# Stick-breaking heads: the value halves held in the array, both halves of the turned weights moving in one matmul

## The reference

```python
def stick_breaking_attention(q, k, v, g):
    scale = SB_HEAD_DIM ** -0.5                      # 64 ** -0.5
    for start in range(0, S, Q_BLOCK):               # blocks of 128 queries
        end = start + Q_BLOCK
        qb, kb, vb = q[:, start:end], k[:, :end], v[:, :end]
        z = jnp.einsum('bqhd,bkhd->bhqk', qb, kb).astype(jnp.float32) * scale
        mask = jnp.arange(end)[None, :] < (start + jnp.arange(Q_BLOCK))[:, None]
        log_1mb = jnp.where(mask, jax.nn.log_sigmoid(-z), 0.0)
        suffix = lax.cumsum(log_1mb, axis=3, reverse=True) - log_1mb
        a = jnp.where(mask, jnp.exp(jax.nn.log_sigmoid(z) + suffix), 0.0)
        outs.append(jnp.einsum('bhqk,bkhd->bqhd', a.astype(vb.dtype), vb))
    o = jnp.concatenate(outs, axis=1)
    return rmsnorm(o, g).reshape(B_, S, SB_WIDTH)
```

## Time and profile before

| what | value |
|---|---|
| median of 3 runs | 3962.36 us |
| lowest and highest | 3954.04 and 3963.06 us |
| span of the profiled execution | 3954.2 us |
| PE busy, share of the span | 3727.1 us, 94% |
| weight loads of PE | 3270.0 us, 83% |
| DVE busy | 1989.4 us, 50% |
| ACT busy | 1700.0 us, 43% |
| POOL busy | 799.3 us, 20% |
| chain that ended last: PE, DVE, ACT | 71%, 12%, 8% |

### The profile page before, as it was taken

How to read it: one execution, slowest core, us unless ns; L and a number is a source line. 1 busy time by engine, 2 the same in 40 slices (tenths; PEclk the granted TensorE clock), 3 DMA queues, 4 the chain that set the end, 5 groups by cost and what they waited for, 6 DMA issues and landing times.

```text
span 3954.2 us, 56218 instructions
## 1 busy us (share of the span) xinstructions
PE 3727.1 (94%) x21768; PEld 3270.0 (83%) x21768; DVE 1989.4 (50%) x4259; ACT 1700.0 (43%) x3455; POOL 799.3 (20%) x704
## 2 busy tenths in 40 slices
PE   7999899999998999999999999999999989999998
PEld 6888788787878887888888987888879987888897
DVE  4446575556646565555646545444566743101343
ACT  4334455556644444445544434334555543111322
POOL 3443333454444331100001000111000000000100
PEclk9999999999999999999999999999999999999999
DMA  6886667676666567454444555555353445555453
GB/s 171 276 270 184 191 206 276 223 266 233 241 238 210 208 208 277 173 174 165 164 171 159 176 192 208 181 181 179 132 201 124 142 157 212 192 192 191 163 187 143
DMA packets 327706, 774.76 MB, mean 196 GB/s; under 512 B 36241, under 2 KB 212369, under 8 KB 271122
## 3 DMA queue, kind: packets, MB, share of 16 engines
q1 hardware_dynamic: 266386, 731.31, 53.2%
q10 hardware_dynamic: 61056, 39.86, 3.6%
HBM read 591.49 MB, written 179.59 MB: 195 GB/s over the span
## 4 chain that ended last, share of the span: by engine, by line
PE 71%; DVE 12%; ACT 8%; issue 3%; DMA 2%; ACTq 2%; POOL 1%; SPq 0%; DVEq 0%
PE PS L1325 19%; PE PS L1327 19%; PE PS L1326 19%; PE PS L1447 3%; PE PS L1433 3%; PE PS L1425 2%; PE PS L1424 2%; PE PS L1449 2%; DVE PT L1967 1%; POOL WF L2225 1%; DVE SM L1935 1%; ACT WF L1547 1%; DVE BIG L1866 1%; ACT PT L1662 1%; ACT BIG L1604 1%
## 5 line engine op out<-in xcount | busy, mean ns | idle before, releaser
L1325 PE MATMUL PS<-WF,BIG 128*128 128x256 f32 (+1 forms) x2328 | 731.8, 314 | 21.1 <-POOL WF L2225 10.5
L1326 PE MATMUL PS<-WF,BIG 128*128 128x256 f32 (+1 forms) x2328 | 715.2, 307 | 0.0
L1327 PE MATMUL PS<-WF,BIG 128*128 128x256 f32 (+1 forms) x2328 | 714.9, 307 | 0.0
L1325 PE MATMUL PS<-BIG,WF 128*128 128x512 f32 (+1 forms) x1792 | 692.3, 386 | 20.4 <-DVE BIG L1866 9.5
L1327 PE MATMUL PS<-BIG,WF 128*128 128x512 f32 (+1 forms) x1792 | 677.7, 378 | 0.0
L1326 PE MATMUL PS<-BIG,WF 128*128 128x512 f32 (+1 forms) x1792 | 677.0, 378 | 0.0
L2225 POOL TENSOR_TENSOR WF<-RAW,WF 128x512 fp32r<-128x512 f32 x380 | 506.9, 1357 | 769.9 <-ACT WF L1547 769.7
L1967 DVE TENSOR_TENSOR PT<-PS,PT 128x512 fp32r<-128x512 f32 (+3 forms) x320 | 194.9, 609 | 616.3 <-ACT PT L1662 615.3
L1325 PEld LDWEIGHTS PS<-WF,BIG 128*128 128x128 f32 x2328 | 453.2, 195 | 48.6 <-POOL WF L2225 9.4
L1326 PEld LDWEIGHTS PS<-WF,BIG 128*128 128x128 f32 x2328 | 453.8, 195 | 22.4 <-issue 2.4
L1327 PEld LDWEIGHTS PS<-WF,BIG 128*128 128x128 f32 x2328 | 453.0, 195 | 18.9
(11 more groups left out here) (220 smaller groups left out, 6809.1 us busy)
## 6 DMA issues: line engine op xcount, KB each, us to landing
WF<-scratch_WS SPq DMA_DIRECT2D x264, 1024.0 KB, 5.1
scratch_WS<-WF SPq DMA_DIRECT2D x110, 1024.0 KB, 6.6
W<-scratch_WS SPq DMA_DIRECT2D x66, 1024.0 KB, 5.0
RAW<-in_w_in SPq DMA_DIRECT2D x84, 512.0 KB, 4.5
KV<-scratch_KS SPq DMA_DIRECT2D x60, 512.0 KB, 6.0
KV<-scratch_VS SPq DMA_DIRECT2D x60, 512.0 KB, 4.7
QQ<-scratch_QS SPq DMA_DIRECT2D x192, 128.0 KB, 4.9
XH<-in_x SPq DMA_DIRECT2D x32, 512.0 KB, 6.3
```

Source lines behind the costliest of these rows:

```text
L1325: pe.matmul(o, Ah, Bh, start=first, stop=False)
L1326: pe.matmul(o, Ah, Bl, start=False, stop=False)
L1327: return pe.matmul(o, Al, Bh, start=False, stop=last)
```

## The change

In the stick-breaking heads the two halves of the values (high, low, 64 columns each, so 128 columns of one head) become the stationary operand, and the two halves of the turned weights move in one matmul of 256 columns. PS[7] then holds, for head r, the output turned: 128 rows (64 of the high values, 64 of the low) by 256 columns (128 queries by the high weights, 128 by the low). So a tile's end gets three steps in place of one: `fold_out` (DVE) adds the two column halves into 256 columns of `PP`, `turn_out` (PE) turns them back with two transposes into PS[6], and `take_turned` (DVE) adds the two halves of the values into `OB`. The turned-back output comes two halves (`FB`) after the fold. The slot of `PP` that the fold writes to is taken from the ring of the logs (seven slots to six). All four products of the halves are now in the sum, three before. The values of the last block are stored with the head outermost, with eight DMAs of 64-column runs in place of four of 128-column runs.

```diff
+FB = 2
@@ attention()
+        fold_after = [(), ()]
@@ weigh(c, x, r, en)
-                _, o_before = oring.take(("o2", c, x["j"], x["qt"]))
-            do(("pv", c, x["x"], r, x["j"], x["qt"], x["kb"], x["w"], x["s"], vslot[c, x["j"], x["kb"]], en, x["first"],
+                _, o_before = oring.take(("o2" if en == 128 else "of", c, x["j"], x["qt"]))
+            do(("pv" if en == 128 else "pv_sb", c, x["x"], r, x["j"], x["qt"], x["kb"], x["w"], x["s"], vslot[c, x["j"], x["kb"]], en, x["first"],
...
                 if x["last"]:
-                    (take_out(c, x, r, en) if c == 0 else in_halves(1, lambda: take_out(c, x, r, en), True))
+                    take = take_out if en == 128 else fold_out
+                    (take(c, x, r, en) if c == 0 else in_halves(1, lambda: take(c, x, r, en), True))
...
+        def fold_out(c, x, r, en):
+
+            j, qt = x["j"], x["qt"]
+            do(("fold_out", c, x["x"], r, j, qt, fold_after[qt % 2]))
+            fold_after[qt % 2] = (("ot", c, j, qt),)
+
+            def turn_back():
+                _, before = tring.take(("o2", c, j, qt))
+                do(("turn_out", c, j, qt, before))
+                do(("take_turned", c, j, qt, ob_after[j % 2]))
+                if qt == 3:
+                    in_halves(1, lambda: finish_head(c, j))
+            in_halves(FB, turn_back)
...
-            aslot, cslot = Ring(7, pch.held[:7]), Ring(3, pch.held[7:])
+            aslot, cslot = Ring(6, pch.held[:6]), Ring(3, pch.held[7:])
+            fold_after[0] = fold_after[1] = pch.held[6]
...
-            pch = Ring(10, aslot.held + cslot.held)
+            pch = Ring(10, aslot.held + [fold_after[0] + fold_after[1]] + cslot.held)
@@ tensor_program(pe)
+            def pv_sb(c, x, r, j, qt, kb, w, s, vs, en, first, last, o_before):
...
+                vv = values_of(vs).rearrange("p (t r m) -> p t r m", t=4, r=2)
+                pp = turned_both(s)
+                o = PS[7][:, 256 * r:256 * r + 256].rearrange("p (a q) -> p a q", a=2)
+                for i in range(w // 128):
+                    m = pe.matmul(o, vv[:, i, r, :], pp[:, :, 128 * i:128 * i + 128],
+                                  start=first and i == 0 and r == 0, stop=last and i == w // 128 - 1, skip_group_check=True)
+                m.then_inc(*inc("weighed", ("pv", x, r)))
+
+            def turn_out(c, j, qt, before):
+                on.wait_ge("of", c, j, qt)
+                for e in before:
+                    on.wait_ge(*e)
+                for r in range(2):
+                    m = pe.transpose(PS[6][:, 128 * r:128 * r + 128], folded(qt)[:, 128 * r:128 * r + 128], ident)
+                m.then_inc(*inc("o_turned", ("ot", c, j, qt)))
@@ scalar_program, put_v
-                        act.dma_start(VS[ft + f, c, :, 2 * g:2 * g + 2, a, :], view.bitcast(F32)).then_inc(*landed(f"s_st{s}", ("qst", u)))
+                        if ft < 4:
+                            act.dma_start(VS[ft + f, c, :, 2 * g:2 * g + 2, a, :], view.bitcast(F32)).then_inc(*landed(f"s_st{s}", ("qst", u)))
+                            continue
+                        by_head = VS[ft + f, c, :, :, :, :].rearrange("p t a e -> p (t a e)").rearrange("p (t r a e) -> p t r a e", t=4, r=2, a=2)
+                        for i in range(2):
+                            act.dma_start(by_head[:, 2 * g + i, :, a, :],
+                                          view[:, i, :].rearrange("p (r e) -> p r e", r=2).bitcast(F32)).then_inc(*landed(f"s_st{s}", ("qst", u)))
@@ vector_program
+            def fold_out(c, x, r, j, qt, before):
+                dst = folded(qt).rearrange("p (r q) -> p r q", r=2)
+                src = PS[7][:, :].rearrange("p (r a q) -> p r a q", r=2, a=2)
+                on.wait_ge("pv", x, r)
...
+                dve.tensor_reduce(dst, src.rearrange("p r a q -> p r q a"), AX, ALU.add).then_inc(*inc("o_step", ("of", c, j, qt)))
+
+            def take_turned(c, j, qt, O_before):
+                dst = outs_of(j)[:, 128 * qt:128 * qt + 128].rearrange("p (r e) -> p r e", r=2)
+                src = PS[6][:, 0:256].rearrange("p (r a e) -> p r a e", r=2, a=2)
+                on.wait_ge("ot", c, j, qt)
...
```

23 lines of the change are left out of this document (18 added, 5 removed).

## The result

The changed kernel takes **4049.4 us** (median of 4 runs, 4046.4 to 4053.7) against 3962.7 for the kernel before, measured beside it: a ratio of 1.023 (95% interval 1.021 to 1.025), 87 us slower. The forecast of 3966 us, with a range up to 3991, was wrong. The profiled execution has a span of 4044.3 us, against 3954.2.

What follows compares the result with a forecast made beforehand. PE, busy 94% of the span, was taken to set the time by what it does in order. The terms -45 + 9 + 18 + 7 + 14 + 5 - 4 = +4 on 3962.4 gave 3966 us, range 3937 to 3991.

Steps and rivals of the forecast that it cites:

- (4): The other 24 turn-backs, chunks 1 to 3: exposed waits for the low half and the later fold, +7 us (3 to 12).
- (2): Turn-backs' own time on PE: 32 tiles with two transposes each, +9 us (8 to 11).
- (6): PE's clock: eight waits over 2 us, every other one bringing the lower clock, +5 us (0 to 12).
- (1): Value matmuls on PE: 544 pieces go from 0.2025 to 0.12 us each, gain 45 us (41 to 50).
- (5): Eight more stores at each chunk's end, issued by ACT and delaying PE: +14 us (6 to 19).
- (3): Chunk 0's turn-backs: PE waits 21.7 us, less 3.6 of present waits; net +18 us (10 to 26).
- if PE's idle time grows elsewhere: Sign on PE's timeline: idle time growing outside the named places would make the forecast as a whole fail.
- (7): Given back: PE's waits let POOL and DVE catch up, so later waits shrink, -4 us (-12 to +2).
- stores at the chunk ends: Rival: sixteen issues hold ACT at four places and PE returns at low clock; 3977 us, chance 0.20.

Runs made afterwards that it cites:

- e4: Changed kernel with run-out halves after the stick-breaking heads charged 10/12 (chunk 0) and 11/13, so the two added halves are paid for: 4004.0 us.
- e2: Changed kernel without its turn-backs, the sum in PS[7] added straight into the output tile, half of the queries left out: 3932.2 us.
- e3: Kernel before with the stick-breaking heads' values stored by eight DMAs in place of four: 3970.9 us.
- e18: Changed kernel with scores in the old places, the fold right behind its value product and the turn-back one half later in every chunk: 3949.2 us.
- e13: Kernel before with attention shifted later by dearer run-out halves, and stick-breaking take_out right behind its value product in chunks 1 to 3: 3996.6 us.
- e14: Kernel before, scores in their old places, with stick-breaking take_out queued right behind its value product in chunks 1 to 3: 3951.3 us.

## Why the prediction was wrong, point by point

Two steps failed. Term (4) priced what the turn-back and the later fold do in chunks 1 to 3 at +7 us; with their own time, (2), that is some 14, and the runs show some 45 there (e4 less e2, by the pairing). And the order of everything that the planner places behind two more halves was put at nothing; e4_place shows 42. The clock term, (6), was 5 where the traces have 28; it followed the number of waits, which these two steps had wrong. Terms (1), (2) and (5) held, and (3) was 8 too small. The last of the prediction's own signs, "if PE's idle time grows elsewhere", came true.

**(1) Value matmuls: right.** 0.12 a piece as said, 45 us. e2_noturn gives -27 together with the stores, and e3 puts those at 11: -38. Of the other 7, e2's trace has 5 us more of waits and 3 more at the low clock than e3's. One reading was off without harm to the sum: the old matmuls did not cost 0.10 "alike" but 0.14 behind one of 128 columns and 0.08 behind one of 64 (starts 1753.08, 1753.23, 1753.31 in the trace). The Trainium skill, TensorE: Matmul & The Clock Gate, section Back-to-back issue gap, gives 81 ns for a pair, by which the gain would be an estimated 29; the trace had 0.10, and the measured 0.12 for the new piece and the -38 side with the trace.

**(2) Turn-backs' own time: right.** There are 64 transposes. Where PE doesn't wait at one (22 tiles of the changed kernel), a turn-back puts the matmuls behind it 0.23 us later, at the median: 7 us for 32, where I said 8.6.

**(3) Waits at chunk 0's turn-backs: right in kind, too small.** The waits are 25.2 us in seven for the low half and 1.5 in the last tile for its own fold, 26.7 where I said 21.7. The third tile's is 7.5 where I took 6, and without DVE catching up gave 7.1: that assumption gave nothing. The value products still wait 2.8 for the low half, and I had let their 3.6 fall away. Net 26 and not 18, the top of the term's bounds.

**(4) The other 24 turn-backs: wrong.** I said +7, and that the fold's later release of PS[7] "counts only where PE waits for it", 10.0 us at three or four places. The turn-backs themselves hardly wait there in the changed kernel (0.7 of 25.9). But the value product waits 34.9 us for the fold, in 13 places. As I read it, three things make it so: PE reaches the next product sooner (14.6 in seven waits in e2_noturn already, with a take of the old size), the fold is longer and the turn-back holds up its queue (18.8 in nine in e4_place), and the shifted order (34.9). Together with (2) and (3) I had 34; e4 less e2 is 72. With the fold and the turn-back placed well it is 18 (e18 less e2), the slot of `PP` included. So the sum of the operations was more than enough for a well placed version, and the place, which I took as given, was worth more than all of it.

**(5) Stores: right.** 11 measured alone, 14 said; PE's waits grew to 5.25 and 5.11, where I said 6.

**(6) Clock: too small.** I counted eight waits over 2 us and 5.5 us. There are 26 more of them, and 28 us more at the lower clock: about 1.1 us for each. The price per wait was somewhat low (0.7 on the mean in my sum), the number of waits far too low.

**(7) Given back: not seen.** No run shows a gain of this kind. In e2_noturn, with a faster PE and no turn-back, the waits are 15 us more than before, and 10 of these e3 has with the stores alone. That a faster PE waits more where DVE is late would explain the other 5; it is argued.

**The missing term.** The shifted order, 42 us here and 70 alone, was in none of my steps, nor in a rival. Both lines that make it are in the text of the change and of the kernel: `in_halves(FB, turn_back)` with `finish_head` behind it, and a run-out that is charged by the half. I followed the added steps and their waits, and never asked what two more halves at a chunk's end do to everything planned after them. The rival "stores at the chunk ends" was on the right side with the wrong mechanism; the range's upper end, 3991, was made from the high ends of the terms that I had, so it could not hold one that I had not.

**What stays open.** Why the shifted order costs what it does is shown in part. With `take_out` early in both orders the shift costs 45 (e13 less e14) and not 73, so 28 of the 73 hang on that step's late place. Of the 45, the traces have 29 in PE's waits, 10 of them for `combine` (L1961: 12.9 us in 5 waits, 2.8 in 2 in e14), and 10 in low clock. That these too are steps queued behind a backlog, like the copy at 1042.00, is argued and not shown. What of the 42 in the changed kernel goes with which step was not tried. That the sweep of five shifts is not even suggests that each order has its own set of meetings, and five points can't show its form. Two slots in PS[7] for the output of the kernel before, which would have taken that wait away in another way, were not tried.

## What to carry to other kernels

When a change makes one stream's chain of steps longer, look first at what else is scheduled by the length of that chain: here two empty halves, charged to a planner, cost 42 of the 87 us, and 70 when nothing else was changed. Where a step frees something that the bound engine waits for, queue it right behind its input and not behind the next block's work, and check that each queue ahead of it can't itself be held up: this was worth some 7 us in the tuned order, 35 in the shifted one, and, with the turn-back moved up behind it, 45 in the changed kernel. And test such a change in the old order too, with the added delay paid for, before it is judged: 4049 and 3949 us are the same operations.
